# Layer one of the MLP in another pair order, with its hand-over to layer two loaded earlier

## The reference, cut to what matters

```python
def post_block(x, mix, ln1_g, ln1_b, w1, w2, ln2_g, ln2_b):
    x = layer_norm(ALPHA * x + mix, ln1_g, ln1_b)
    h = jnp.square(jax.nn.relu(x @ w1)) @ w2
    return layer_norm(ALPHA * x + h, ln2_g, ln2_b)
```

## Time and profile before

| | us |
|---|---|
| median of 3 executions | 1391.93 |
| lowest and highest | 1386.42, 1395.73 |
| profiled execution, its own time | 1392.48 |
| its span | 1390.8 |
| PE busy (92% of the span) | 1285.3 |
| DVE busy (61%) | 847.3 |
| ACT busy (41%) | 565.4 |
| mean DMA rate over the span | 165 GB/s |

### The profile page before, as it was taken

One profiled execution on the slowest core, in us unless ns is written; L12 is line 12 of the kernel. 1 busy time (PEld: TensorE's weight loads), 2 busy tenths in 40 slices (PEclk: granted clock), 3 DMA queues, 4 the chain that ended last, 5 costly groups with the idle time before them and its releaser, 6 DMA issues. The chain is left out here.

```text
span 1390.8 us, 24860 instructions
## 1 busy us (share of the span) xinstructions
PE 1285.3 (92%) x9826; PEld 1200.5 (86%) x9826; DVE 847.3 (61%) x1357; ACT 565.4 (41%) x932; POOL 173.1 (12%) x216
## 2 busy tenths in 40 slices
PE   7999999999978997899979999999977999999896
PEld 7987778887756776899979999999977999999896
DVE  4112221545685776566776777777746666668978
ACT  3213232233634444634644444454444333333425
POOL 3424343010000000032100000000000000000553
PEclk9999999999789999999989999999989999999998
DMA  8658887422300002143224776676689655554103
GB/s 289 215 164 283 278 280 243 126 69 87 121 8 19 10 1 91 43 152 96 77 70 159 258 274 223 247 266 231 233 311 361 237 185 186 184 185 162 61 5 119
DMA packets 110809, 229.85 MB, mean 165 GB/s; under 512 B 12723, under 2 KB 60101, under 8 KB 106086
## 3 DMA queue, kind: packets, MB, share of 16 engines
q1 hardware_dynamic: 104550, 211.48, 44.1%
q0 software_dynamic: 6144, 16.79, 3.8%
HBM read 167.39 MB, written 60.84 MB: 164 GB/s over the span
## 5 line engine op out<-in xcount | busy, mean ns | idle before, releaser
L2676 PE MATMUL psum<-step_hid_hi,step_w_hi 128*128 128x258 f32 x784 | 162.1, 289 | 22.7 <-ACT y_sums L2692 6.8
L2676 PE MATMUL psum<-step_hid_hi,step_w_lo 128*128 128x258 f32 x784 | 160.6, 287 | 0.0
L2676 PE MATMUL psum<-step_hid_lo,step_w_hi 128*128 128x258 f32 x784 | 160.4, 287 | 0.0
L355 PE MATMUL psum<-xTh,win_hi 128*128 128x344 f32 (+1 forms) x432 | 148.9, 345 | 9.7 <-DVE xTl L408 9.7
L2676 PEld LDWEIGHTS psum<-step_hid_hi,step_w_hi 128*128 128x128 f32 x784 | 125.2, 195 | 23.9 <-DVE step_hid_lo L2645 7.0
L355 PE MATMUL psum<-xTh,win_lo 128*128 128x344 f32 (+1 forms) x432 | 140.6, 325 | 0.0
L355 PE MATMUL psum<-xTl,win_hi 128*128 128x344 f32 (+1 forms) x432 | 140.5, 325 | 0.0
L2676 PEld LDWEIGHTS psum<-step_hid_hi,step_w_lo 128*128 128x128 f32 x784 | 124.5, 194 | 0.0
L2676 PEld LDWEIGHTS psum<-step_hid_lo,step_w_hi 128*128 128x128 f32 x784 | 124.3, 194 | 0.0
L2366 PE MATMUL psum<-x_t_hi,w_variant_hi 128*128 128x258 f32 x512 | 105.1, 287 | 9.5 <-DVE product_sums L2458 5.9
L2366 PE MATMUL psum<-x_t_lo,w_variant_hi 128*128 128x258 f32 x512 | 105.0, 287 | 0.0
(11 more groups left out here) (416 smaller groups left out, 3048.2 us busy)
## 6 DMA issues: line engine op xcount, KB each, us to landing
hid_rows<-hid_variants SPq DMA_DIRECT2D x14, 1806.0 KB, 6.9
step_hid_raw<-hid_rows SPq DMA_DIRECT2D x21, 1032.0 KB, 7.6
k_pages<-in_pages SPq DMA_DIRECT2D x128, 160.0 KB, 3.1
v_pages<-in_pages POOLq DMA_DIRECT2D x128, 128.0 KB, 4.6
w_raw<-in_w SPq DMA_DIRECT2D x16, 1024.0 KB, 5.2
step_w_raw<-w_sums SPq DMA_DIRECT2D x12, 1024.0 KB, 5.2
step_w_raw<-in_w SPq DMA_DIRECT2D x9, 1024.0 KB, 5.1
win_raw<-in_w_in SPq DMA_DIRECT2D x17, 512.0 KB, 7.1
```

What stands on the lines that cost most here:

```text
L355: mm = pe.matmul(psum[0:M, 3 * (m % 2) + b, 0:BLK], w[:, m % 2, k, 0:M], x[:, k, b * BLK:(b + 1) * BLK], start=(k == 0 and i == 0), stop=( ...
L2676: mm = pe.matmul(slot(d)[:, s, :], wt[r][:, w], ht[r][:, TH * f + s * BW:TH * f + (s + 1) * BW], start=(f == 0 and i == 0), stop=(f == G - ...
```

## The change

- Pairs go in their own order 0 to 15, so the two pairs without sums (14 and 15) come last in layer one. Their four blocks each stay in `hv` (variants 0 to 3 and 4 to 7) until the end reads them there; their stores and `last_hid_raw` are gone.
- Pairs 0 and 1 now get variants: the hidden sums of pair n - 1 are made in turns 1 to 14, not 3 to 15 and in layer two. Their stores are of 1806 KB and wait for `hid_t4`.
- The sums of w2 for pair q are made in turn q + 2, and the w2 loads and stores move up with them.
- SyncE's last part of layer one loads steps 1, 0 and 2 and the residual quarters of P5 and P3; step 0 has a staging tile of its own, in the part of `hv` that pair 13 leaves, and waits for the store of pair 13; step 2's load waits for step 0's. The other two quarters follow in layer two.

```diff
         def load_w1(sp, n):
-            sp.dma_start(w1in[n % 2][:], a["w1"][PAIRS[n]]).then_inc(st_loaded[n % 2], 16)
+            sp.dma_start(w1in[n % 2][:], a["w1"][n]).then_inc(st_loaded[n % 2], 16)
...
-        PAIRS = [14, 15, *range(14)]
-        NP, NE = len(PAIRS), 4
+        NP, NE = DFF // (2 * P), 4
+        NW = NP - 2
...
         def h_view(n, v):
-            return hv[:, n % 2, v, :]
+            return hv[:, 4 + v if n == NP - 1 else 7 * (n % 2) + v, :]
...
-                if n >= 3 and p == "P6":
+                if 0 < n <= NW and p == "P6":
                     hid_t3_t1(dve, n - 1)
-                if n >= 3 and p == "P7":
+                if 0 < n <= NW and p == "P7":
                     hid_t2(dve, n - 1)
-                if n >= 3 and p == "P4":
+                if 0 < n <= NW and p == "P4":
                     hid_t4(dve, n - 1)
-                if n >= 3 and p in turn_order(n)[:3]:
-                    w2_sums(dve, n - 3, turn_order(n).index(p))
+                if n >= 2 and p in turn_order(n)[:3]:
+                    w2_sums(dve, n - 2, turn_order(n).index(p))
...
         def store_hid(sp, n):
-            if n < 2:
-                sp.wait_ge(sq_done, 4 * n + 4)
-            else:
-                sp.wait_ge(hv_done, n - 1)
-            w = 4 if n < 2 else 7
-            sp.dma_start(hvs[PAIRS[n], :, 0:w * TH].rearrange("p (v c) -> p v c", v=w), hv[:, n % 2, 0:w, :]).then_inc(hv_stored[n % 2], 16)
+            sp.wait_ge(hv_done, n + 1)
+            sp.dma_start(hvs[n].rearrange("p (v c) -> p v c", v=7), hv[:, 7 * (n % 2):7 * (n % 2) + 7, :]).then_inc(hv_stored[n % 2], 16)
...
         def sp_hidden(sp):
-            for n in range(NP):
+            for n in range(NP - 1):
                 if n + 2 < NP:
                     sp.wait_ge(mwa_lo, AT[n, "P3"] + 1)
                     load_w1(sp, n + 2)
-                if n == NP - 1:
-                    sp_step_load(sp, 0)
-                if n >= 3:
-                    store_w2(sp, n - 3)
                 if n >= 2:
-                    load_w2(sp, n - 2)
-                if n == NP - 1:
-                    sp_step_load(sp, 1)
+                    store_w2(sp, n - 2)
                 if n:
+                    load_w2(sp, n - 1)
                     store_hid(sp, n - 1)
+            sp_step_load(sp, 1)
+            sp_step_load(sp, 0)
+            store_w2(sp, NW - 1)
+            sp_step_load(sp, 2)
+            sp.wait_ge(u_c_done, u2_at(NP - 1))
+            load_z(sp, 0, "P5", XHALF[1], slice(TH, T))
+            sp.wait_ge(w2s_stored, GLA_ROWS_IN + 32 * NW)
+            load_z(sp, 1, "P3", XHALF[0], slice(TH, T))
...
             if x == 0:
-                sp.wait_ge(mwa_lo, AT[NP - 2, "P3"] + 1)
+                sp.wait_ge(hv_stored[1], GLA_ROWS_IN + 16 * (NW // 2))
             elif x == 1:
+                sp.wait_ge(mwa_lo, AT[NP - 1, "P1"] + 1)
+            elif x == 2:
                 sp.wait_ge(mwa_lo, NPROD)
+                sp.wait_ge(st_loaded[0], ST_BASE + 32)
...
-                if x == 0:
-                    hid_t3_t1(dve, NP - 1)
-                    hid_t2(dve, NP - 1)
-                    hid_t4(dve, NP - 1)
-                    for part in range(3):
-                        w2_sums(dve, NP - 3, part)
...
-                act.activation(hch[:, k, :], hn[:, k // 2, k % 2 * T:(k % 2 + 1) * T], ACT.Copy).then_inc(pb_hi, 1)
+                act.activation(two(hch[:, k, :]), hid_tile(k), ACT.Copy).then_inc(pb_hi, 1)
```

More of the change, by code:

```diff
@@ L2217, in hymba_step @@
         HV_B11, HV_B12, HV_B21, HV_B22, HV_T2, HV_T3, HV_T4 = range(7)
-        hv = sb(PERSIST, "hid_variants", [P, 2, 7, TH])
+        hv = sb(PERSIST, "hid_variants", [P, 14, TH])
         w2low = sb(PERSIST + 7224, "w2_left_half", [P, 2, 512])
@@ L2509, in load_w2 @@
             else:
-                sp.wait_ge(sq_done, 8)
+                sp.wait_ge(sq_done, 1)
                 sp.wait_ge(u_c_done, u2_at(1))
@@ L2568, in hymba_step @@
                               for n, off, w in (("hid_hi", 0, 4 * TH), ("hid_lo", 4 * TH, 4 * TH), ("w2_hi", 8 * TH, 2048), ("w2_lo", 8 * TH + 2048, 2048)))
-        STAGE = [AREA, PERSIST]
+        STAGE = [AREA, PERSIST + 4 * T + 8]
         stw = [sb(at_s, f"step_w2_raw{i}", [P, 2048]) for i, at_s in enumerate(STAGE)]
         sth = [sb(at_s + 2048, f"step_hid_raw{i}", [P, 4 * TH]) for i, at_s in enumerate(STAGE)]
-        stw0 = [sb(AREA + 2056 * i, f"step_w2_first{i}", [P, 1024]) for i in range(2)]
-        sth0 = [sb(AREA + 2056 * i + 1024, f"step_hid_first{i}", [P, 2 * TH]) for i in range(2)]
-        sth00 = sb(AREA + 26296, "step_hid_very_first", [P, 2 * TH])
+        FIRST = [PERSIST + 4 * T, AREA, AREA + 2056]
+        stw0 = [sb(at_s, f"step_w2_first{i}", [P, 1024]) for i, at_s in enumerate(FIRST)]
+        sth0 = [sb(at_s + 1024, f"step_hid_first{i}", [P, 2 * TH]) for i, at_s in enumerate(FIRST)]
+        assert STAGE[1] + 4112 <= PERSIST + KD * T and 4 * T + 1024 + T <= 7224
         def staging(x):
             if x < 7:
-                return stw0[x % 2], sth0[x % 2] if x else sth00
+                i = 1 + (x - 1) % 2 if x else 0
+                return stw0[i], sth0[i]
             return stw[x % 2], sth[x % 2]
@@ L2695, in dve_steps @@
             A = {p: acc_of(p) for p in ORDER}
-            Z_OF = {"P5": 1, "P4": 2, "P2": 3, "P3": 4}
+            Z_OF = {"P5": 1, "P3": 2, "P4": 3, "P2": 4}
             def joined(p, q, n):
@@ L2748, in hymba_step @@
         NC = 4
-        hn = sb(PERSIST + 4112, "last_hid_raw", [P, 2, 2 * T])
-        wmean = sb(PERSIST + 8240, "w2_row_means", [P, 8])
+        wmean = sb(PERSIST + 4 * T, "w2_row_means", [P, 8])
         w2c = sb(STAGE[0], "last_w2_raw", [P, 2, 2, 2, 512])
@@ L2758, in hymba_step @@
         ysum = sb(ln_at, "y_column_sums", [P, T])
-        assert 4112 + 4 * T + 8 <= PERSIST + KD * T and VR_AT[0] + KD * T <= 53200
+        assert VR_AT[0] + KD * T <= 53200
         HC_BASE, WC_BASE = PB + 2 * NS, PB + 2 * NS + NC
@@ L2763, in sp_steps @@
         def sp_steps(sp):
-            def load_z(i, p, ks, c):
-                if i:
-                    sp.wait_ge(zb_loaded, ONE_IN + 16 * i)
-                sp.dma_start(acc_of(p), zs[:, ks, c]).then_inc(zb_loaded, 16)
-            t1, t2 = slice(0, TH), slice(TH, T)
-            for x in range(2, NS):
-                if x == 7:
-                    sp.wait_ge(hv_stored[1], GLA_ROWS_IN + 16 * (NP // 2))
-                if x == LAST7:
-                    sp.wait_ge(w2s_stored, GLA_ROWS_IN + 32 * (NP - 2))
+            for x in range(3, NS):
@@ L2794, in w2c_tile, with hid_tile @@
         def w2c_tile(t, k):
             return t[:, k // 2, :, k % 2, :]
+        def hid_tile(k):
+            return hv[:, 2 * k:2 * k + 2, :]
         def hid_split_hi(act):
-            act.wait_ge(w1early_loaded, ONE_IN + 48)
+            act.wait_ge(sq_done, 4 * NP)
             act.wait_ge(y_mm, PB + 4 * (NS - 2))
             for k in range(NC):
-                act.activation(hch[:, k, :], hn[:, k // 2, k % 2 * T:(k % 2 + 1) * T], ACT.Copy).then_inc(pb_hi, 1)
+                act.activation(two(hch[:, k, :]), hid_tile(k), ACT.Copy).then_inc(pb_hi, 1)
@@ L2810, in hid_split_lo @@
                 dve.wait_ge(pb_hi, HC_BASE + k + 1)
-                dve.tensor_tensor(hcl[:, k, :], hn[:, k // 2, k % 2 * T:(k % 2 + 1) * T], hch[:, k, :].bitcast(F32), ALU.subtract).then_inc(pb_lo, 1)
+                dve.tensor_tensor(two(hcl[:, k, :]), hid_tile(k), two(hch[:, k, :]).bitcast(F32), ALU.subtract).then_inc(pb_lo, 1)
         def w2c_split_hi(act):
```

24 lines of the change are left out of this document (9 added, 15 removed).

## The result

| | before | changed |
|---|---|---|
| median (us) | 1392.25 (7 executions) | 1380.86 (7 executions) |
| lowest, highest | 1386.42, 1395.73 | 1374.71, 1386.08 |
| profiled execution, span | 1392.48, 1390.8 | 1376.08, 1374.4 |

The ratio of the changed kernel's time to that of the kernel before is 0.9913, 95% interval 0.9888 to 0.9939: 11.4 us, or about 0.9%. A later comparison of the same two kernels gave 0.9939 (0.9912 to 0.9965). The forecast was 1381.5 us.

What follows compares the result with a forecast made beforehand. PE bounds layer one's steady turns; 25.8 us are lost at the hand-over to idle PE and low clock. 1392.5 - 20 + 9.8 = 1382.3, the median 0.6 lower, given as 1381.5; forecast 1378 to 1386, range 1374 to 1390.

Steps and rivals of the forecast that it cites:

- Hand-over: Layer one to layer two: shorter queue and earlier step loads remove PE's waits, so step 7 starts 20 us sooner.
- Turn 3: Layer one: pair 1's hidden store lands late, 10.8 us after issue, so PE waits 7.1 us on L2458.
- Turn 2: Layer one: six extra w2 sums ahead of L2458 on DVE delay PE's P4, a loss of 1.5 us.
- The clock: Behind turn 3's wait in layer one: PE runs at the slow rate for a while, costing 1.6 us.
- Turn 4's wait of 1.12 us stays: Layer one: turn 4's w2 store and load keep their distance from P4 of turn 3, so PE's 1.12 us wait remains.
- Sum of the front: First turns of layer one: 1.5 + 7.1 - 0.4 + 1.6, a loss of 9.8 us, bounds 4 to 12.
- A: Turn 3: pair 1's store lands early, PE waits 3.1 us, clock holds; loss 4.2 us, time 1376; chance 0.2.
- B: Hand-over: step 2 lands at 1018, L2467 stays 6 us late; gain 13 us, time about 1389; chance 0.15.
- C: Hand-over: queue stays slow, some 14 us a small load; gain 8 us only, time 1394; chance 0.08.
- D: Hand-over gain in full, 25.8 us less 3, with a cheap start losing 4.2; time 1374; chance 0.07.
- the bare 40.5 us: Start of layer two: PE time for seven steps of 24 matmul pairs at the full rate, without waits.

Runs made afterwards that it cites:

- the seventh experiment: Changed kernel with w2 sums, their loads and stores a turn back, and three residual quarters loaded in layer two again: 1382.16 us, ratio 0.9930.
- experiments 3 to 6: Changed kernel with, in order: two extra copies (1396.39 us); steps 1 and 2 issued late (1378.10); turn 3's square later (1373.82); turn 2's w2 sums later (1386.86).
- the two repeats: On one chip, the changed kernel with pair 3's first square two products later (1373.34 us, ratio 0.9864), and the changed kernel unedited (1383.70 us, 0.9939).
- experiments 6 to 9: On changed kernel: turn 2's w2 sums later (1386.86 us); w2 sums a turn back (1382.16); back only early, then catching up (1380.40); that plus a store swap (1376.03).
- Experiment 2: Changed kernel with hidden pair 1's store ahead of the w2 load in turn 2, and w2 sums later in turns 3 and 4: 1381.28 us, ratio 0.9934.
- store ahead: Kernel whose w2 sums start at the old distance and catch up, with turn 8's w2 store and load put ahead of the hidden store: 1376.03 us, ratio 0.9877.

## Why the prediction was right, point by point

- **Hand-over, 20 us forecast: 21.0 measured.** Step 7 came 45.25 us behind the start (46 forecast). L2465 and L2467 run at 1019.42 and 1022.30 without holding PE. Against the start, steps 3 and 5 went out at 1.9 and 13.3 us (1.7 and 13.1 forecast) and step 7 at 22.6 (23.6 forecast). From step 7's issue (1041.72) to its start are 22.6 us, as before. The copies cost 0.5 us (0.7 forecast), DVE's adds 3.2 (3). Three parts of the hand-over were put back one at a time: with 7.4 MB of reads and writes put back the distance is 57.7 us, with late steps 49.6, with the w2 work a turn back 58.8. The prediction spoke above all of missing traffic. That is only half of it: the seventh experiment has nearly the changed kernel's bytes and loses 13.5 us to places in SyncE's order.
- **Turn 3, 7.1 us forecast: 6.74.** The term rested on one row, a store of 1806 KB landing 10.8 us after its issue when a w2 load goes just ahead. It came out at 10.8, and at 10.7 to 11.0 in the six other runs with this order (experiments 3 to 6 and the two repeats); alone it took 5.7, ahead of the load 7.8. The 4.6 us from the landing to the end of L2458 stayed 4.6 (763.2 to 767.8).
- **Turn 2, 1.5 us forecast: 1.14.** It is gone wherever fewer or no w2 sums stand ahead of L2458 in that turn (experiments 6 to 9).
- **The clock, 1.6 us forecast: near 1.9.** Ten rows from 768.53 to 772.40 came every 0.43 us instead of 0.24.
- **"Turn 4's wait of 1.12 us stays": wrong.** It is gone, though its premise held: the second halves of w2's store and load went out 2.05 and 6.01 us behind P4 of turn 3 in both kernels (765.43 and 769.39 behind 763.38 before), and L2458 of turn 4 started 20.8 us behind it before and 20.9 now.

```profile
770.01 0.43 SPq L2518 DMA_DIRECT2D w_sums<-w_right_half  x1
773.97 0.43 SPq L2513 DMA_DIRECT2D w_right_half<-in_w  x1
```

```profile
788.85 0.70 DVE L2458 TENSOR_TENSOR product_sums<-psum,product_sums 128x516 f32<-128x516 f32 x1
```

```profile
790.47 0.41 PE L2366 MATMUL psum<-x_t_hi,w_variant_hi 128*128 128x258 f32 x2
```

What failed is the sum: the slow clock behind turn 3's wait, which the same forecast counts, made PE itself some 2 us later at P4 of turn 4 (22.5 us behind P4 of turn 3, before 21.6 with the wait in it), and the wait of 1.12 us vanished inside that. The two were added where they overlap. The runs bear it out: where turn 3 waited over 5 us and the slow rate followed, turn 4 waited for nothing; where it waited 0.41 to 2.6 us and the clock held, 1.05 to 1.23 us are back. (Experiment 2 moved turn 4's own sums and is no case of either.)
- **Sum of the front: 9.8 forecast, 8.9 measured.** The second wait of turn 0 (5.25 us against 4.38) is in it, which no term had. It is 4.38 in two kernels with the changed front, 4.48 in "store ahead" and 5.2 to 5.6 in the others, the one with the sums a turn back among them, so it says nothing of the change. This 0.87 us more and turn 4's 1.12 us less happen to offset each other.
- **Total.** 21.0 - 8.9 + 0.7 is 12.8 us, the forecast 10.2, the medians give 11.4. That 1380.86 lies within a microsecond of 1381.5 is partly luck: the recorded execution alone, with its early start, was 1376.08, and the repeat has a median of 1383.70.
- **The rivals.** A (store lands early, 1376) fell with the 10.8 us, B (step 2 late) and C (slow queue) with the missing waits: step 2's two loads, issued at 1011.82 and 1012.23, took 4.7 and 5.7 us. But waits of the kind that B and C describe are what experiments 3 and 7 show, at 12 to 14 us each, so they were rivals of the right kind. D's full gain did not come: 4.75 us above the bare 40.5 us remain at the hand-over.

## What to carry to other kernels

A DMA's landing time here was that of its place in the queue: the same store took 10.8 us just behind a load, 6.8 with the load some 5 us ahead and 5.7 alone. Before moving one, write down what is issued in the 5 us ahead of it, and take the duration from a row with the same neighbour. Where a landing can't be made earlier, look for the first instruction that waits for it and for what is queued behind that instruction; here moving one square behind two conversions did at least as well as any reordering of the transfers (own stretches of 667.6 and 668.1 us against 669.2 for the best of the others). And a schedule that runs a turn ahead moves its cost to where the lead is built up, so look there for slack first: experiment 9 built the lead up in the steady turns and gave back 4.5 of 6.9 us. And a sum of losses needs a look at which of them overlap: a PE that runs slower reaches the next wait later, and the wait shrinks by as much.
